# First modulation group loaded and multiplied in two column halves, and the input projection begun on four of eight chunks

## The reference, cut to what matters

```python
def adaln(cvec, w, b):
    m = jax.nn.silu(cvec) @ w + b          # w: 1024 x 6144
    ...                                    # sh1, sc1, g1, sh2, sc2, g2, 1024 columns each

sh1, sc1, g1, sh2, sc2, g2 = adaln(cvec, lp['w_mod'], lp['b_mod'])
h = modulate(rms_norm(x, lp['norm1']), sh1, sc1)     # h * (1 + sc1) + sh1
z = h @ lp['w_in']                                   # columns: q, k, v, xr, gb
```

## Time and profile before

| | |
|---|---|
| median of 3 runs | 641.57 us |
| the three runs | 636.82, 641.57, 643.0 us |
| the profiled execution | 639.3 us, of which the span of the profile is 637.4 us |
| PE, DVE, ACT, POOL busy | 592.1 (93%), 351.4 (55%), 176.5 (28%), 94.9 us (15%) |
| mean granted clock of TensorE | 0.984 |
| chain that ended last | PE 73%, DMA 14%, DVE 6%, ACT 3%, SPq 2% |

### The profile page before, as it was taken

One profiled execution on the slowest core, in us unless ns is written; L12 is line 12 of the kernel. 1 busy time (PEld: TensorE's weight loads), 2 busy tenths in 40 slices (PEclk: granted clock), 3 DMA queues, 4 the chain that ended last, 5 costly groups with the idle time before them and its releaser, 6 DMA issues.

```text
span 637.4 us, 9407 instructions
## 1 busy us (share of the span) xinstructions
PE 592.1 (93%) x3289; PEld 329.9 (52%) x3290; DVE 351.4 (55%) x784; ACT 176.5 (28%) x369; POOL 94.9 (15%) x131
## 2 busy tenths in 40 slices
PE   0889999899999899999999989999999999789797
PEld 0344544455656677645555545555555554355452
DVE  2475698755654988754666784334333343413437
ACT  4202687701123777741111100110110110000000
POOL 4000011121133100000000111122221222201200
PEclk9979999899999999999999999999999999979999
DMA  8999543350008908809312949999999999999877
GB/s 340 396 348 390 192 148 139 115 214 1 1 9 241 353 2 211 373 28 409 125 67 99 375 169 385 418 418 419 418 419 412 419 419 421 419 419 418 358 269 281
DMA packets 45689, 176.26 MB, mean 277 GB/s; under 512 B 10836, under 2 KB 18000, under 8 KB 31192
## 3 DMA queue, kind: packets, MB, share of 16 engines
q1 hardware_dynamic: 34416, 154.86, 61.9%
q0 software_dynamic: 6688, 15.58, 7.0%
q10 hardware_dynamic: 4552, 5.38, 2.4%
HBM read 163.32 MB, written 21.16 MB: 289 GB/s over the span
## 4 chain that ended last, share of the span: by engine, by line
PE 73%; DMA 14%; DVE 6%; ACT 3%; SPq 2%; issue 2%; DVEq 0%; POOLq 0%; ACTq 0%
PE ps L1632 16%; PE ps L1449 11%; DMA expert_w<-exp_w_up 10%; PE ps L1399 8%; PE ps L1387 7%; PE ps L1648 7%; DMA w<-w_mod 4%; PE ps L1487 4%; PE ps L1514 4%; PE ps L1496 3%; PE ps L1600 2%; PE ps L1337 2%; PE ps L1363 2%; PE ps L1550 1%; PE ps L1692 1%
## 5 line engine op out<-in xcount | busy, mean ns | idle before, releaser
L1632 PE MATMUL ps<-expert_w,hT_mixT 128*64 128x256 f32 x1120 | 136.3, 393 | 11.7 <-DMA expert_w<-exp_w_up 11.4
L1632 PEld LDWEIGHTS ps<-expert_w,hT_mixT 128*64 128x64 f32 x1120 | 84.2, 136 | 67.1 <-issue 23.3
L1387 PE MATMUL ps<-hT_mixT,w 128*128 128x512 f32 (+1 forms) x256 | 74.2, 445 | 1.5 <-DVE hT_mixT L874 1.5
L1449 PE MATMUL ps<-w,hT_mixT 128*128 128x512 f32 x160 | 71.9, 597 | 0.0
L1648 PE MATMUL ps<-expert_w,w 128*64 128x512 f32 x280 | 65.8, 599 | 0.0
L709 ACT ACTIVATE w<-ps 128x128 f32<-128x128 f32 x36 | 10.0, 277 | 193.3 <-PE ps L1632 193.3
L1251 DVE SCALAR_TENSOR_TENSOR w<-w,ps 128x128 f32<-128x128 f32 x36 | 10.3, 287 | 87.0 <-ACT w L709 87.0
L1387 PEld LDWEIGHTS ps<-hT_mixT,w 128*128 128x128 f32 x256 | 39.8, 195 | 35.2 <-issue 33.4
L1269 DVE TENSOR_TENSOR w<-ps,w 128x1024 f32<-128x1024 f32 x18 | 22.0, 1224 | 59.9 <-PE ps L1648 59.9
L1399 PE MATMUL ps<-w_qkv,hT_mixT 128*128 128x512 f32 (+1 forms) x160 | 53.1, 488 | 0.0
L1449 PEld LDWEIGHTS ps<-w,hT_mixT 128*128 128x128 f32 x160 | 29.1, 191 | 29.8 <-issue 29.6
(11 more groups left out here) (277 smaller groups left out, 757.7 us busy)
## 6 DMA issues: line engine op xcount, KB each, us to landing
expert_w<-exp_w_down SPq DMA_DIRECT2D x31, 1024.0 KB, 19.3
expert_w<-exp_w_gate SPq DMA_DIRECT2D x29, 1024.0 KB, 15.0
expert_w<-exp_w_up SPq DMA_DIRECT2D x29, 1024.0 KB, 17.7
w_mod_ring<-w_mod SPq DMA_DIRECT2D x18, 1024.0 KB, 7.3
y_rows<-zero_rows POOLq DMA_DIRECT2D x10, 512.0 KB, 9.2
expert_w<-y_rows SPq DMA_DIRECT2D x10, 512.0 KB, 7.8
recurrence<-w_mod SPq DMA_DIRECT2D x4, 1024.0 KB, 12.5
w<-w_in SPq DMA_DIRECT2D x4, 1024.0 KB, 16.6
```

The costliest lines, as they stand in the source:

```text
L1387: ins = pe.matmul(ps[:, bank, 0:n], w1v[:, c, m * P:(m + 1) * P], HM[:, c, lo:lo + n], start=(c == 0), stop=(c == DC - 1))
L1449: ins = pe.matmul(ps[:, 2 * (t % 2) + half, :], HM[:, c, t * P:(t + 1) * P], w1v[:, c, half * 512:(half + 1) * 512], start=(c == 0), stop= ...
L1632: ins = pe.matmul(ps[r, 2 + k, 0:2 * P].rearrange("p (k f) -> p k f", k=2), xT[:, c, r], gate_up(i)[:, :, c, k:FF:FC], start=(c == 0), sto ...
```

## The change

The first group is loaded, multiplied and turned in two column halves, and the projection begins on the four chunks of `HM` that the first half allows.

- **Halves.** Half 0 is quarters 0 and 2 (columns 0 to 511 of `sh1` and of `sc1`), half 1 quarters 1 and 3. Each chunk becomes two DMAs of 512 KB (`w_mod_columns`), and `w_in(0)` is put between the halves, `w_in(1)` behind them, ahead of chunks 8 and 9.
- **Products.** `first_modulation(c, half)` takes two chunks, c and c+1, at a time: four matmuls for two chunks by two quarters, each into its own 32 rows of bank 0. There are 32 matmuls in the first group, as before. The even and the odd chunks' sums stay apart, and a 128x4 matrix of ones (`pairsum`) adds them while it turns them (`mod_turn`: four matmuls of four columns with the rows as stationary operand). DVE adds the bias to the columns, which the bias rows in `prow` now bring (one small DMA more, `R_BM`).
- **PE's order.** Four matmuls on the first tokens are put at the head, whose result isn't used. Then half 0 between the `x_turn`s, `mod_turn(0)`, the first four chunks of `z(0)`, half 1 in two pieces around the first chunks of `z(1)`, `mod_turn(1)`, and the last four chunks of `z(0)` and `z(1)` around chunks 8 and 9. `z(1)` part 1 gets bank 6.
- **DVE's order.** `decay()` stands between the modulating of the halves.
- The first group's rows are no longer written to memory; ACT's loads wait for the last column halves instead.

```diff
-            for n in range(DC):
-                w_mod(n)
+            for c in range(DC):
+                w_mod_columns(c, 0)
             w_in(0)
+            for c in range(DC):
+                w_mod_columns(c, 1)
+            w_in(1)
             w_mod(DC)
             w_mod(DC + 1)
-            w_in(1)
-            sp.wait_ge(S["mod_mm"], DC)
+            sp.wait_ge(S["mod_mm"], 1 + DC // 2)
             w_in(2)
             w_in(3)
             w_mod(DC + 2)
...
+            def first_modulation(c, half):
+
+                if half and c == 0:
+                    pe.wait_ge(S["mod_ev"], 1)
+                pe.wait_ge(*(other_columns_in if half else first_columns_in)(c))
+                for o in range(2):
+                    for k in range(2):
+                        quad = 32 * (2 * o + k)
+                        ins = pe.matmul(ps[quad:quad + 32, 0, :], csil[:, c + o, :], w_mod_place(c + o)[:, 2 * k + half, :],
+                                        start=(c == 0), stop=(c == DC - 2))
+                if half or c == DC - 2:
+                    ins.then_inc(S["mod_mm"], 1)
+
+            def mod_turn(half):
+
+                pe.wait_ge(S["mod_ev"], half + 1)
+                for b in range(4):
+                    ins = pe.matmul(ps[:, 7, 4 * b:4 * b + 4], msb[:, b * P:(b + 1) * P], pairsum, start=True, stop=True)
+                ins.then_inc(S["mrow_t"], 1)
+            pe.wait_ge(rows_in[0], 16)
+            for _ in range(4):
+                pe.matmul(ps[:, 5, :], ident[:, :], X[:, 0, 0:512], start=True, stop=True)
             pe.wait_ge(S["csil"], 2)
...
+            def first_mod_rows(half):
+
+                dve.wait_ge(S["mod_mm"], 1 + DC // 2 if half else 1)
+                dve.tensor_copy(msb[:, :], ps[:, 0, :]).then_inc(S["mod_ev"], 1)
...
+            modulate(0)
             decay()
+            first_mod_rows(1)
+            mod_columns(1)
+            modulate(1)
```

More of the change, by code:

```diff
@@ L259, in chain @@
             return step
+        pairsum = small[:, C_SUM:C_SUM + 4]
         def w_mod_place(n):
@@ L849, in decay, with xn_out @@
                 dve.tensor_scalar(small[:, C_KAP:C_KAP + 8], acc, 2.0, None, ALU.mult).then_inc(S["lru_par"], 1)
-            for t in range(NT):
+            def xn_out(t):
                 dve.wait_ge(S["xnT"], t + 1)
@@ L867, in _ @@
-            for v in range(2):
-                step(dve.scalar_tensor_tensor(out=mcol[:, v, 1, :], in0=mcol[:, v, 1, :], scalar=1.0,
-                                              in1=par[:, R_N1:R_N1 + 8], op0=ALU.add, op1=ALU.mult))
+                dve.wait_ge(S["mod_mm"], 1 + DC // 2 + g * DC)
+                if g == 1:
+                    dve.wait_ge(S["bm_in"], 32)
+                else:
+                    dve.wait_ge(S["mod_out"], 32)
+                dve.tensor_tensor(msb[:, :], ps[:, 0, :], bm[:, g - 1, :], ALU.add).then_inc(S["mod_ev"], 1)
@@ new lines, in modulate @@
+            def modulate(half):
+                for c in range(4 * half, 4 * half + 4):
+                    for v, lo, n in ((1, 0, LAT), (0, LAT, CTX)):
+                        dve.tensor_scalar(HM[:, c, lo:lo + n], HM[:, c, lo:lo + n], mcol[:, v, 1, c:c + 1],
+                                          mcol[:, v, 0, c:c + 1], ALU.mult, ALU.add).then_inc(S["hT"], 1)
+            for t in range(NT - 1):
+                xn_out(t)
+            first_mod_rows(0)
+            xn_out(NT - 1)
+            mod_columns(0)
@@ L1331, in modulation @@
                 g, c = n // DC, n % DC
[L1332 to L1335, removed]
+                if c == 0:
+                    pe.wait_ge(S["mod_ev"], g + 1)
+                w = w_mod_place(n)
+                pe.wait_ge(*later_group_in(n))
                 for q in range(4):
@@ L1339, in modulation @@
                 ins.then_inc(S["mod_mm"], 1)
-            pe.wait_ge(S["csil"], 2)
[L1341 to L1352, removed]
+            def first_modulation(c, half):
[17 more added lines that the diff above has]
+                pe.matmul(ps[:, 5, :], ident[:, :], X[:, 0, 0:512], start=True, stop=True)
+            pe.wait_ge(S["csil"], 2)
+            first_modulation(0, 0)
+            pe.wait_ge(S["par_in"], 16 * 8)
+            pe.wait_ge(S["par_c"], 1)
+            pe.transpose(ps[:, 7, 0:ROWS], prow[0:ROWS, :], ident[0:ROWS, 0:ROWS]).then_inc(S["par_t"], 1)
+            x_turn(0)
+            first_modulation(2, 0)
+            x_turn(1)
+            x_turn(2)
+            first_modulation(4, 0)
+            x_turn(3)
+            first_modulation(6, 0)
+            x_turn(4)
+            mod_turn(0)
             def gates(u):
@@ L1361, in gates @@
                 for k in range(2):
+                    if u == 0 and k:
+                        pe.wait_ge(S["z_ev"], 4)
                     for lo, n in ((0, LAT), (LAT, CTX)):
@@ L1382, in z @@
                         pe.wait_ge(w1_in[m // 2], 16)
-                    free(j, part)
+                    if m >= 2:
+                        free(j, part)
                 for c in chunks:
@@ L1411, in turn @@
                 ins.then_inc(S["qT"], 1)
[L1412 to L1416, removed]
+            fore, aft = range(DC // 2), range(DC // 2, DC)
+            z(0, 0, fore)
+            z(0, 1, fore)
+            first_modulation(0, 1)
+            first_modulation(2, 1)
+            z(1, 0, fore)
+            first_modulation(4, 1)
+            first_modulation(6, 1)
+            z(1, 1, fore)
+            mod_turn(1)
+            z(0, 0, aft)
+            z(0, 1, aft)
+            modulation(DC)
+            modulation(DC + 1)
+            z(1, 0, aft)
+            z(1, 1, aft)
+            gates(0)
+            modulation(DC + 2)
+            modulation(DC + 3)
+            for m in range(2, 6):
+                z(m, 0, fore)
+                gates(2 * (m - 2) + 1)
+                z(m, 0, aft)
                 z(m, 1)
-                if 1 <= m <= LC:
+                if m <= LC:
                     gates(2 * (m - 1))
```

84 lines of the change are left out of this document (44 added, 40 removed).

## The result

The changed kernel is slower: 643.07 us median of 18 runs (639.92 to 645.43) against 639.02 us of 18 runs of the kernel before (636.32 to 644.21), a ratio of 1.0058 with a 95% interval of 1.0035 to 1.008. That is 3.7 us, or 2.2 to 5.1. The forecast was 2.0 us faster. The profiled execution has a span of 641.9 us, 4.5 more than before.

What follows compares the result with a forecast made beforehand. DMA was taken to bound the start. Of 4.5 us gained at `gates(0)`, chunk 11's landing left 2.6, and the clock's 0.6 left 2.0: 640.2 - 2.0 = 638.2 us, 8 in 10 range 634 to 643.

Steps and rivals of the forecast that it cites:

- What bounds, and at which point the gain is decided: Start bound by DMA; PE meets chunks 10 and 11, whose product ends at 59.4 instead of 61.97, leaving 2.6 us.
- The rate of the halves: Column halves in 2 KB pieces at 386 GB/s: first halves in at 21.6 us, other halves at 35.5.
- The slower rival: Halves load below 344 GB/s, chunk 11 lands late, PE starves: 3.0 us slower, 643.2 us; chance 0.13.
- PE up to `gates(0)`: PE's sum from the start: `z(0)` at 27.0 us, 9.9 earlier; `gates(0)` done at 55.6, 4.5 earlier.
- The step that failed: Chunk 8 requested near 38 us, with `w_in(1)` and ACT's gate weights still on their way: wait costed at nothing.
- The other term of the sum that failed with it: Loads from `w_in(1)` to chunk 11 take 23.0 us as before, so chunk 11 lands at 58.5 us.
- The clock: Low-clock stretches of PE at `z(0)` or chunk 11, mostly paid by slack: 0.6 us taken off the gain.
- "nothing": Rival: PE cold at `z(0)` and `z(1)`, chunk 8 requested late, DMAs dry for 2 us: 640 us; chance 0.17.
- The bound of the slower side: Upper end of the 8 in 10 range, set by the slower rival: 643 us.
- What passes on: Stages behind chunk 11, from `gates(1)` to attention and experts, move by the same amount; nothing absorbs the gain.

Runs made afterwards that it cites:

- e4: Changed kernel with four unused 128x512 products on PE between `gates(0)` and chunk 10: 640.88 us, ratio 1.0028 to the kernel before.
- e1: Changed kernel with half 1 of chunks 4 to 7 multiplied ahead of `z(1)` part 0, the second turning behind it: 641.22 us, ratio 1.0042 to the kernel before.
- e3: Changed kernel with own places for chunks 8 and 9, and chunks 10 and 11 loaded ahead of `w_in(2)` and `w_in(3)`: 639.65 us, ratio 1.0013 to the kernel before.

## Why the prediction was wrong, point by point

**What bounds, and at which point the gain is decided: right.** The forecast rested on PE meeting chunks 10 and 11, and that is where the loss is.

**The rate of the halves: right.** I had the first halves in at 21.6, `w_in(0)` at 24.6 and the other halves at 35.5 us. The last of them landed at 35.4, which is 0.2 us behind the same bytes in the kernel before (35.2). The slower rival, in the form that I gave it (the halves below 344 GB/s), didn't occur: 374 GB/s and more. On this the Trainium skill, "DMA: Bandwidth & Descriptors", section "Bandwidth" (batch to 1 MiB or more for three quarters of the peak), is not borne out for DMAs in a full queue: 512 KB each, they moved at 378 GB/s from 16.5 to 22 us.

**PE up to `gates(0)`: off by 1.3 us.** `z(0)` began at 29.1 for 27.0. `x_turn(0)` waited for DVE to 16.6 where I had put it near 15, and the granted clock fell to 0.51 for 5.5 us. `mod_turn` cost 0.8 to 1.0 us for my 1.6. `gates(0)` began at 54.7 for 53.4. Chunk 9, which I had in by 47 at the latest, landed at 48.8, 0.6 us ahead of its product.

**The step that failed** is the one on the request of chunk 8: "At that time `w_in(1)` and ACT's gate weights are still on their way, so I cost this wait at nothing". The time of the request was nearly right (near 38; it was 40.2, as `z(0)` began 2.1 us late). What was wrong is that enough would still be on its way. All but 0.06 MB of `w_in(1)` had been moved by 37.5 us, and ACT's small pieces, then nearly alone, kept the DMAs at 127 GB/s until chunk 8's bytes arrived. To the hole of 3.0 us the request's own delay belongs: some 2 us from asking until the rate is back, which a full queue hides. The term at nothing measured 3.0 us.

The other term of the sum that failed with it is the 23.0 us from `w_in(1)` to chunk 11, taken from landing to landing in the kernel before; it measured 27.7. The two stretches (before, then changed):

```profile
35.20:58.20 23.00, 21.45 (x82) 11.06 (x82) 16.97 (x63) 1.68 (x4) 0.00 (x0) 0.90 1.07 356
```

```profile
35.40:63.10 27.70, 22.52 (x108) 10.51 (x104) 17.16 (x45) 5.47 (x9) 0.00 (x0) 0.93 0.93 322
```

They hold 8.20 and 8.93 MB. At 356 GB/s the 0.73 MB more are 2.1 us, and the lower rate, in which the hole lies, is 2.6 us. A landing is the time of a load's last byte, and doesn't say how much of the loads behind it has been moved by then; two landings don't bound the same bytes in both kernels. Sum: chunk 11 at 63.1 for 58.5, its product's end at 65.1 for 59.4.

**The clock: undersized.** I took 0.6 us. Behind PE's wait for chunk 10 the mean clock of 57 to 65 us was 0.65, and e4's profile prices it at 1.6 us.

**The rivals.** What happened is "nothing" in mechanism (PE late at chunks 4 and 5, chunk 8 asked for late, the DMAs dry, chunk 11 late), with 0.17 of the chance and a price of 2 us of dry DMAs for the measured 3.0. I had tied the late request to a cold PE at `z(0)`, where 40.2 us, with `z(0)` and `z(1)` at full clock, was late enough. The bound of the slower side, 643.0, was 0.1 us too low.

**What passes on.** The shift did arrive at the end: 3.15 us at `z(2)`, 3.7 at the first product of w_qkv, 3.7 in the ratio. The products of w_qkv, before and in the changed kernel:

```profile
124.73 5.85 PE L1399 MATMUL ps<-w_qkv,hT_mixT 128*128 128x512 f32 x13
```

```profile
128.45 1.98 PE L1463 MATMUL ps<-w_qkv,hT_mixT 128*128 128x512 f32 x4
```

**Still open:** why the DMAs were thin from 49 to 51 us in the one profiled execution of the changed kernel, with `w_in(2)` and `w_in(3)` already asked for; no run tells its cause. What an earlier request for chunk 8 is worth by itself: e1 gave 1 us in the runs against 2.7 in its profile, and e3 moved chunks 10 and 11 ahead in the list as well. A version that only frees chunk 8's place earlier, with the order of the loads and of PE's products kept, wasn't run.

## What to carry to other kernels

When a buffer is reused, moving its consumer later on the compute engine moves the next request later as well. Beside the order of the loads, work out for each request the moment at which it is made, and compare it with the moment at which the queue ahead of it runs empty. A transfer time taken from a stretch with two queues at work holds only for that mix; once the large loads are gone, small ones can't keep the DMAs busy (127 GB/s here). And when a wait for data can't be avoided, put a stage there that doesn't need the data: two moved lines of PE's list won back 4.4 us with the loads as late as they were. The gains don't add up: once the loads were in time, the same move gave 1.5 us more, within the noise.

## What the runs showed of the hardware that I had not expected

- From 37.5 to 42 us ACT's loads in small pieces (gate weights, tables) had hardly anything beside them, and the DMAs moved 127 GB/s, with a DMA share of 0.61. Beside 1 MB loads the same stretch moved 407 GB/s (e3), and then they came in at 58 us, 3.2 us after they were needed.
- A 1 MB load (chunk 8) asked for while only such pieces moved took 5.5 us to land; in a full queue such loads follow each other every 2.6 us. Its first bytes moved 1.0 to 1.3 us after it was asked for, and from 42 us on the rate is back:

```profile
42.00:44.00 2.00, 0.95 (x10) 0.86 (x8) 1.04 (x4) 0.00 (x0) 0.00 (x0) 1.00 0.91 350
```

  The Trainium skill, "DMA: Bandwidth & Descriptors", section "Anatomy of one DMA — SWDGE (gpsimd) path", gives some 2 us fixed for a DMA of POOL's kind. This one is SP's; its 5.5 us are 2.9 more than the 2.6, which is of that size, though no run here separates the fixed part.
- Before its low stretch in the changed kernel PE had stood for 2.8 and 2.1 us with 1.3 us of work in between; the granted clock was then 0.51 from 16.5 to 22 us. Around its wait of 3.6 us at chunk 10 it was 0.65 over eight microseconds.
